# First stage of a fused decoder block: modulation columns loaded in blocks that pair shift and scale, tiles scaled and multiplied block by block

## What is computed

```python
c_act = jax.nn.silu(c)
mod = c_act @ w_mod[l] + b_mod[l]                 # 1024 -> 6 * 1024
sh1, sc1, g1, sh2, sc2, g2 = jnp.split(mod, 6, axis=-1)
h = _modulate(_rmsnorm(x, norm1_gain[l]), sh1, sc1)   # xhat * gain * (1 + sc1) + sh1
...
proj = h @ w_in                                   # 1024 -> 2372 columns
# index scores: idx_q @ idx_k, relu, weighted by idx_w, summed over 4 heads; top 256 keys of each query
# stick-breaking attention (8 heads), sparse attention (8 heads, the kept keys), output projection
x = x + g1 * mixer(h)
h = _modulate(_rmsnorm(x, norm2_gain[l]), sh2, sc2)
x = x + g2 * _swiglu(h, w_gate, w_up, w_down)
return _modulate(_rmsnorm(x, final_gain), sh_f, sc_f)
```

## Time and profile before

| | us |
|---|---|
| median of 3 runs | 1480.56 (1479.33 to 1481.61) |
| the profiled execution | 1475.04 |
| its span in the trace | 1473.3 |
| busy: PE, DVE, ACT, POOL | 1337.3, 1025.8, 680.1, 737.1 |
| mean granted TensorE clock | 0.964 of full |

### The profile page before, as it was taken

How to read it: one execution, slowest core, us unless ns; L and a number is a source line. 1 busy time by engine, 2 the same in 40 slices (tenths; PEclk the granted TensorE clock), 3 DMA queues, 4 the chain that set the end, 5 groups by cost and what they waited for, 6 DMA issues and landing times.

```text
span 1473.3 us, 18364 instructions
## 1 busy us (share of the span) xinstructions
PE 1337.3 (91%) x6085; PEld 1057.6 (72%) x6085; DVE 1025.8 (70%) x1478; ACT 680.1 (46%) x1132; POOL 737.1 (50%) x677
## 2 busy tenths in 40 slices
PE   1689999995999998895998899999999999999997
PEld 1556888784666666563886678888888888887885
DVE  4858579999677655543476997666666666477787
ACT  4435577744677655553213833332333334254332
POOL 1153355464456568875001245555555556487552
PEclk9798899996999999997899999999999999999999
DMA  8680134445444233220664245444444446889432
GB/s 335 191 225 18 58 129 135 136 157 151 113 115 115 57 110 85 72 60 22 256 210 134 76 141 184 150 149 152 152 156 161 156 150 219 321 297 322 166 114 115
DMA packets 124265, 223.33 MB, mean 152 GB/s; under 512 B 9322, under 2 KB 52436, under 8 KB 123924
## 3 DMA queue, kind: packets, MB, share of 16 engines
q1 hardware_dynamic: 124180, 222.27, 45.8%
HBM read 160.90 MB, written 57.93 MB: 149 GB/s over the span
## 4 chain that ended last, share of the span: by engine, by line
PE 41%; DVE 7%; issue 2%; DMA 1%; ACT 1%; POOL 0%; DVEq 0%; POOLq 0%; ACTq 0%
PE ps_out L2196 25%; PE ps_out L2222 12%; PE ps_out L1533 2%; PE ps_out L1549 1%; DVE mod_acc_final L1616 1%; DMA scr_mod_final<-mod_acc_final 1%; DVE y_full L1637 1%; DVE wgu_lo L2303 0%; ACT square_junk L2114 0%; DVE x L2458 0%; DVE y_gated L1649 0%; DVE down_part L2456 0%; DVE h_sum_t L2270 0%; DVE h_t_full L2270 0%; DVE x L2480 0%
## 5 line engine op out<-in xcount | busy, mean ns | idle before, releaser
L1893 POOL TENSOR_TENSOR wgu_lo<-wgu_raw,wgu_hi 128x512 fp32r<-128x512 f32 x66 | 97.2, 1481 | 127.7 <-ACT wgu_hi L1885 127.7
L2130 POOL TENSOR_TENSOR dn_lo<-dn_raw,dn_hi 128x512 fp32r<-128x512 f32 x77 | 126.3, 1658 | 67.7 <-ACT dn_hi L2036 67.7
L1885 ACT ACTIVATE wgu_hi<-wgu_sum 128x512 fp32r<-128x512 f32 x88 | 55.2, 632 | 199.0 <-DVE wgu_sum L2286 80.0
L2196 PE MATMUL ps_out<-h_b_t_hi,wgu_hi 128*128 128x512 f32 x352 | 137.9, 392 | 6.6 <-DVE h_b_t_lo L2274 2.7
L2196 PE MATMUL ps_out<-h_b_t_hi,wgu_lo 128*128 128x512 f32 x352 | 137.7, 391 | 0.0
L2196 PE MATMUL ps_out<-h_b_t_lo,wgu_hi 128*128 128x512 f32 x352 | 137.6, 391 | 0.0
L2036 ACT ACTIVATE dn_hi<-dn_raw 128x1024 fp32r<-128x1024 f32 x77 | 81.2, 1062 | 114.4 <-PE ps_out L2222 55.4
L413 POOL TENSOR_TENSOR win_lo<-win_raw,win_hi 128x256 fp32r<-128x256 f32 (+1 forms) x84 | 62.2, 771 | 136.5 <-ACT win_hi L404 136.5
L2222 PE MATMUL ps_out<-dn_hi 128*128 128x512 f32 x308 | 120.2, 390 | 0.0
L2222 PE MATMUL ps_out<-dn_hi,dn_lo 128*128 128x512 f32 x308 | 119.8, 389 | 0.0
L2222 PE MATMUL ps_out<-dn_lo,dn_hi 128*128 128x512 f32 x308 | 119.8, 389 | 0.0
(11 more groups left out here) (326 smaller groups left out, 3659.1 us busy)
## 6 DMA issues: line engine op xcount, KB each, us to landing
scr_act_sums<-act_sums SPq DMA_DIRECT2D x11, 1792.0 KB, 6.8
dn_raw<-scr_act_sums SPq DMA_DIRECT2D x77, 256.0 KB, 5.2
wgu_raw<-in_w_gate_dram SPq DMA_DIRECT2D x11, 1024.0 KB, 5.3
wgu_raw<-in_w_up_dram SPq DMA_DIRECT2D x11, 1024.0 KB, 5.3
wd_sums<-in_w_down_dram SPq DMA_DIRECT2D x11, 1024.0 KB, 5.0
scr_wd_sums<-wd_sums SPq DMA_DIRECT2D x11, 1024.0 KB, 4.1
dn_raw<-scr_wd_sums SPq DMA_DIRECT2D x44, 256.0 KB, 7.0
win_raw<-in_w_in_dram SPq DMA_DIRECT2D x20, 512.0 KB, 4.4
```

The lines of the kernel that those rows point to most:

```text
L1893: pool.tensor_tensor(sl[slot(m, x)][:], src, sh[slot(m, x)][:].bitcast(F32), ALU.subtract).then_inc(wlp, 1)
L2130: pool.tensor_tensor(bl[q % NSLOT][:, 1], braw[entry(q)][:, 1], bh[q % NSLOT][:, 1].bitcast(F32), ALU.subtract).then_inc(dlw, 1)
L2196: last = pe.matmul(bank(m, b), a[s][:, t], h[x][t // 2][:, t % 2], start=(fresh and t == 0 and a is sh and h is hh), stop=(t == 3 and a is ...
```

## The change

The blocks of `w_mod` are cut anew: block j now holds 256 columns of the shift and the same 256 features' scale, so that two feature groups can be scaled once one block is summed. A block arrives as two pieces of rows 0 to 5 of the eight slabs (`KV_` = 6) and two of rows 6 and 7, each with 256 columns. DVE's chain covers six slabs; PE takes the last two with eight more matmuls of one column against `csil` (`column_sums`). ACT makes the factors of each block from PSUM (`factors`, four operations of one column) instead of DVE. The `x` tiles 0 to 3 and the first two column tiles of `w_in` are loaded ahead of all blocks. The sixteen steps run in another order (`steps`), four of them ahead of blocks 2 and 3 on DVE, with three transpose buffers instead of four. The 16 steps of `mod_acc_early` leave the loop and stand behind it, with the other 16. Tile 2 of `w_in` is split into buffers of its own (`win2_hi`, `win2_lo`), its rounding on ACT is moved into the first stage, and its load and that of tile 3 stand ahead of `load_mod(0)`. Block buffer 0 now lies in `score`, so `load_mod(0)` waits for block 2.

```diff
-        for j in range(4):
+        def load_x(half):
+            for i in range(4 * half, 4 * half + 4):
+                sp.dma_start(xt[:, i, :], xb[i]).then_inc(x_loaded[i], 16)
+
+        def load_columns(j):
             if j >= 2:
-                for i in range(4 * j - 8, 4 * j - 4):
-                    sp.dma_start(xt[:, i, :], xb[i]).then_inc(x_loaded[i], 16)
                 sp.wait_ge(accd, j - 1)
-            sp.dma_start(wm[j % 2][:], w_mod[:, :, 512 * j:512 * j + 512]).then_inc(wm_loaded[j % 2], 16)
+                sp.wait_ge(modm, j - 1)
+            for t0, t1, done in ((0, KV_, wm_loaded), (KV_, KD, wp_loaded)):
+                for x in range(2):
+                    c = D * x + 256 * j
+                    sp.dma_start(wm[j % 2][:, t0:t1, 256 * x:256 * x + 256],
+                                 w_mod[:, t0:t1, c:c + 256]).then_inc(done[j % 2], 16)
+
+        load_x(0)
         then.first_loads(sp)
+        load_columns(0)
+        load_columns(1)
+        load_x(1)
+        load_columns(2)
+        load_columns(3)
...
+        then.first_highs(act)
+        factors(0)
+        modulate(0)
+        modulate(1)
+        square(4)
+        square(5)
+        factors(1)
+        modulate(2)
+        modulate(3)
+        square(6)
+        square(7)
         for i in range(4, NT):
             normalise(i)
-        then.first_highs(act)
-        for n in range(2 * KD):
+        factors(2)
+        for n in range(4, 12):
+            modulate(n)
+        factors(3)
+        then.third_high(act)
+        for n in range(12, 2 * KD):
             modulate(n)
...
+        column_sums(0)
+        for n in range(NTS):
+            transposes(n)
+        column_sums(1)
+        for n in range(2 * KD):
+            then.first_products(pe, n, *steps[n])
+            if n == 3:
+                column_sums(2)
+            if n + NTS < 2 * KD:
+                transposes(n + NTS)
+            if n == 5:
+                column_sums(3)
         pe.wait_ge(const_ready, 7)
-        for n in range(2 * KD):
-            if n + 4 < 2 * KD:
-                transposes(n + 4)
-            then.first_products(pe, n)
...
+        column_chain(0)
+        column_chain(1)
+        for n in range(4):
+            split(n)
+        column_chain(2)
+        column_chain(3)
+        for n in range(4, 2 * KD):
+            split(n)
         dve.wait_ge(const_ready, 7)
...
         def first_loads(sp):
-            sp.wait_ge(before.accd, 3)
             for n in range(2):
                 load_weights(sp, 0, n)
...
+            load_weights(sp, 0, 2)
+            load_weights(sp, 0, 3)
+            sp.wait_ge(before.accd, 3)
+            sp.wait_ge(before.modm, 3)
             load_mod(0)
             load_mod(1)
-            load_weights(sp, 0, 2)
-            load_weights(sp, 0, 3)
             for n in range(2, 7):
                 load_mod(n)
             stack_q(0)
...
             for n in range(3):
-                weights_high(act, 0, n + 2)
+                if n:
+                    weights_high(act, 0, n + 2)
                 evac(0, n, 0.125 if n < 2 else 1.0)
...
-            for m in range(2 * KD, 4 * NF):
+            for m in range(4 * NF):
                 modulation_step(dve, m)
```

More of the change, by code:

```diff
@@ L205, in normalise, with factors @@
             act.activation(xt[:, i, :], xt[:, i, :], ACT.Copy, scale=rstd[:, i:i + 1]).then_inc(xh, 1)
+        def factors(j):
+            act.wait_ge(modm, j + 1)
+            if j == 0:
+                act.wait_ge(abp, 1)
+            for t in range(2 * j, 2 * j + 2):
+                m = ps_m[:, 4 * j + t % 2:4 * j + t % 2 + 1]
+                act.activation(g.b1[:, t:t + 1], m, ACT.Identity, bias=g.cols[:, t:t + 1]).then_inc(ab, 1)
+                m = ps_m[:, 4 * j + 2 + t % 2:4 * j + 3 + t % 2]
+                act.activation(g.a1[:, t:t + 1], m, ACT.Identity, bias=ab1[:, t:t + 1],
+                               scale=g.cols[:, R_N1 + t:R_N1 + t + 1]).then_inc(ab, 1)
         def modulate(n):
-            t = n % KD
+            half, t = steps[n]
             act.wait_ge(tr, n + 1)
-            act.wait_ge(ab, 2)
+            act.wait_ge(ab, 4 * (t // 2 + 1))
             if n >= 2:
                 act.wait_ge(los, n - 1)
-            act.activation(hf[:, n % 2], ps_t[:, n % 4], ACT.Identity,
+            act.activation(hf[:, n % 2], ps_t[:, n % NTS], ACT.Identity,
                            bias=g.b1[:, t:t + 1], scale=g.a1[:, t:t + 1]).then_inc(hfs, 1)
@@ L235, in transposes, with column_sums @@
         def transposes(n):
-            half, t = n // KD, n % KD
+            half, t = steps[n]
             pe.wait_ge(xh, 4 * half + 4)
-            if n >= 4:
-                pe.wait_ge(hfs, n - 3)
+            if n >= NTS:
+                pe.wait_ge(hfs, n - NTS + 1)
             for i in range(4):
-                m = pe.transpose(ps_t[:, n % 4, P * i:P * i + P],
+                m = pe.transpose(ps_t[:, n % NTS, P * i:P * i + P],
                                  xt[:, 4 * half + i, P * t:P * t + P], g.ident[:])
             m.then_inc(tr, 1)
-        for n in range(4):
-            transposes(n)
-        for j in range(4):
-            pe.wait_ge(accd, j + 1)
-            for t in range(4):
-                m = pe.matmul(ps_m[:, 4 * j + t:4 * j + t + 1], acc[:, j, P * t:P * t + P],
-                              g.ones[:, 0:1], start=(j == 0 and t == 0), stop=True,
-                              skip_group_check=True)
-            m.then_inc(modm, 1)
+        def column_sums(j):
+            if j == 0:
+                pe.wait_ge(csil_ready, 1)
+            else:
+                pe.wait_ge(ab, 4 * j)
+            pe.wait_ge(wp_loaded[j % 2], 32 * (j // 2 + 1))
+            for t in range(KV_, KD):
+                for c in range(4):
+                    pe.matmul(ps_m[:, 4 * j + c:4 * j + c + 1], wm[j % 2][:, t, P * c:P * c + P], g.csil[:, t:t + 1],
+                              start=(j == 0 and t == KV_ and c == 0), stop=True, skip_group_check=True)
+            pe.wait_ge(accd, j + 1)
+            for c in range(4):
+                m = pe.matmul(ps_m[:, 4 * j + c:4 * j + c + 1], acc[:, j, P * c:P * c + P], g.ones[:, 0:1],
+                              start=False, stop=True, skip_group_check=True)
+            m.then_inc(modm, 1)
+        column_sums(0)
+        for n in range(NTS):
+            transposes(n)
+        column_sums(1)
[7 more added lines that the diff above has]
+                column_sums(3)
         pe.wait_ge(const_ready, 7)
-        for n in range(2 * KD):
-            if n + 4 < 2 * KD:
-                transposes(n + 4)
-            then.first_products(pe, n)
     def vector(dve):
@@ L401, in weights_high @@
             act.wait_ge(raw_loaded[n % 2], i * 8 + 16 * (n // 2 + 1))
+            if n == T_IKW:
+                act.activation(w2h[:, :, 0:w], raw[:, n % 2, :, 0:w], ACT.Copy).then_inc(whi, 1)
+                return
             if n >= 2:
@@ L409, in weights_low @@
             pool.wait_ge(whi, i + (n + 1))
-            if n >= 2:
+            if n >= 2 and n != T_IKW:
                 pool.wait_ge(proj, i + (n - 1))
+            high, low = (w2h, w2l) if n == T_IKW else (wh[:, n % 2], wl[:, n % 2])
             for t in range(0, KD, 2):
-                last = pool.tensor_tensor(wl[:, n % 2, t:t + 2, 0:w], raw[:, n % 2, t:t + 2, 0:w],
-                                          wh[:, n % 2, t:t + 2, 0:w].bitcast(F32), ALU.subtract)
+                last = pool.tensor_tensor(low[:, t:t + 2, 0:w], raw[:, n % 2, t:t + 2, 0:w],
+                                          high[:, t:t + 2, 0:w].bitcast(F32), ALU.subtract)
             last.then_inc(wlo, 1)
         def first_loads(sp):
-            sp.wait_ge(before.accd, 3)
             for n in range(2):
@@ L678, in project @@
                 s, m = n % 2, width(n)
-                tile_products(pe, ps_p[0:m, s], wh[:, s, :, 0:m], wl[:, s, :, 0:m], g.hTh, g.hTl).then_inc(proj, 1)
+                high, low = (w2h, w2l) if n == T_IKW else (wh[:, s], wl[:, s])
+                tile_products(pe, ps_p[0:m, s], high[:, :, 0:m], low[:, :, 0:m], g.hTh, g.hTl).then_inc(proj, 1)
             project(0, 2)
```

62 lines of the change are left out of this document (31 added, 31 removed).

## The result

The changed kernel is slower. Its median is 1490.3 us (1488.6 to 1492.9) beside 1480.3 (1479.3 to 1481.6) for the kernel before: a ratio of 1.0069, 95% interval 1.0051 to 1.0086. The profiled executions took 1488.6 and 1475.0, with spans of 1486.9 and 1473.3.

A forecast was written before the change was run, and what follows sets the result against it. DVE's key selection bounds the end, its start set by ACT's first relu (111.32). Tile 4 landing at 104.1 instead of being rounded at 93.06 adds 11.0 us: 1480.56 + 11.0 = 1491.6 us; range 1483.5 to 1498.0.

The forecast's parts named there:

- Packets of 1 KB: First-stage block transfers: 354 GB/s, between 289 and 398; last block's slabs 0 to 5 landed at 43.4 us.
- The third rival: First-stage blocks come at the rate of small packets, 289 GB/s: 5.0 us more, 1496.6 us; 15 in 100.
- The last chain ends at 47.8: DVE's last block sum ends at 47.8 us instead of 46.3; step 4 starts on PE at 48.9.
- The steps 0 to 3 fit on PE between 33 and 43: First stage on PE: the first four steps were taken to fit between 33 and 43 us.
- The cover that I had put at 3 us: Squares and normalising of tokens 512 and up end near 45 us, 3 us ahead of need.
- The other steps on PE: PE's steps 4 to 15 take 20.6 us, last `column_sums` 2.7, slow-clock start 1.2; PE ends at 73.4.
- The early sum: DVE's 32 steps begin at 71.3 us, behind the last split; piece 6 is issued at 92.2, 12.3 us later.
- Tile 4: Tile 4 of `w_in`, queued behind piece 6 on SP, lands at 104.1 us; the chain begins 11 us later.
- Tile 4 to relu: From ACT's rounding of tile 4 to its first relu: stays 18.3 us, putting the relu at 122.4.
- The first rival: PE still gates tile 4: relu up to 7.7 us earlier, 1472.9 us, faster; one in ten.
- the second (made up downstream): Rival: the delay is made up after the relu, in DVE's slack in the search: 1480.6 us, same; 5 in 100.
- frees nothing there: Taking early steps out of the split loop saves no time, since PE's pace of 1.83 us was the slower.

The follow-up runs named there:

- steps_in_loop: Changed kernel with 14 of the 16 moved early steps put back between the splits: 1480.5 us, ratio 1.0011 to the kernel before.
- transpose3_early: Changed kernel with PE's transposes for step 3 ahead of the products of step 0: 1491.9 us, ratio 1.0081 to the kernel before.
- first two attempts at a cure: tile4_first and both_cures, which issue loads of `w_in` tiles earlier on SP: 1493.0 and 1477.3 us.
- three later orders tried here: tile4_first, after_queue and kidx_first, the changed kernel with other orders on SP's queue: 1493.0, 1488.3 and 1492.2 us.
- tile4_first: Changed kernel with the load of tile 4 of `w_in` moved ahead of `load_mod(2)` on SP: 1493.0 us, ratio 1.0095 to the kernel before.
- kidx_first: Changed kernel with after_queue's order on SP, but tile 5 and `double_k` ahead of pieces 6 and 7: 1492.2 us, ratio 1.0089.
- both_cures: steps_in_loop with tile 4 ahead of `load_mod(4)` and tile 5 ahead of `load_mod(7)`, `stack_q(1)` and `double_k` on SP: 1477.3 us, ratio 0.9995.
- early_stack: steps_in_loop with SP reordered: tile 4 ahead of piece 4, `stack_q(0)` ahead of piece 6, tile 5 and `stack_q(1)` ahead of piece 7: 1473.9 us.
- after_queue: Changed kernel with only SP's order changed, `stack_q(0)` and tile 4 ahead of pieces 4 and on: 1488.3 us, ratio 1.0060.
- before_steps_out: Kernel before with one part of the change alone, all 32 early steps behind the last split: 1493.9 us, ratio 1.0114.
- before_tile5_first: Kernel before with the load of tile 5 of `w_in` ahead of `double_k()` on SP: 1474.9 us, ratio 0.9970.
- early_stack_t3: early_stack plus the edit of transpose3_early: 1470.9 us, ratio 0.9960 to the kernel before.

## Why the prediction was right, and where it was not

Forecast 1491.6, measured 1490.3, inside the range, and slower as said. By its steps:

- **Packets of 1 KB**: 354 GB/s taken, 347 to 350 read in the timeline's stretches of after (34 to 36 us: 349, share 1.11). The last block's rows were there by about 44, forecast 43.4: DVE waits for them in steps_in_loop and starts at 44.08, and starts without a wait at 43.88 in transpose3_early. The third rival (the rate of 512-byte packets) is out. So is, once more, the rule of the Trainium skill ("DMA: Bandwidth & Descriptors", Specifications) that 512 bytes reach the line rate: 289, 349 and 398 GB/s for 512 bytes, 1 KB and 2 KB are three different rates in these two kernels.
- **"The last chain ends at 47.8", "The steps 0 to 3 fit on PE between 33 and 43"**: this is the step that failed. The chain ended at 49.87 and step 4 started at 51.23 instead of 48.9. I had looked at block 3's landing and at PE's room, not at DVE's own queue: chain 2 stands behind split 3, and that waited for a scaling whose transposes stood on PE behind the half-rate products of step 0. Moving four instructions took 1.6 of these 2.1 us away; the other 0.5 is the block, which landed that much later than said. The cover that I had put at 3 us was gone as well: ACT normalised the last tile of `x` at 48.3, not near 45, and split 4 waited 0.15 us for ACT behind chain 3.
- **The other steps on PE**: 24.5 us from step 4 on (20.6 + 2.7 + 1.2), measured 24.9 (51.23 to 76.1).
- **The early sum**: from the last split to piece 6, 20.9 us forecast (71.3 to 92.2), 20.7 measured (73.90 to 94.6). This was the longest sum of the prediction and it is right to 0.2 us.
- **Tile 4**: 11.9 us from piece 6's issue to the rounding, measured 12.6.
- **Tile 4 to relu**: 18.3 against 18.1. **Relu to the end**: 1:1 (1362.0 us before, 1361.5 after).

In the traces the relu is 14.0 us late where I had 11.0: 2.3 for step 4 and 0.7 for tile 4, with the small misses of the other terms (+0.4, -0.2 and -0.2) cancelling. In the medians the difference is 10.0. So the nearness of 1491.6 to 1490.3 is in part luck: two errors of 3 and 4 us with opposite sign. The second is the spread between executions of one kernel (before: 1475.0 in the profiled one, 1479.3 to 1481.6 in the others). The traces show some of it where nothing is changed: from the start of the search to the end it is 1334.3 to 1342.3 us in the twelve kernels.

The first rival (PE still gates tile 4) is refuted by the releaser at 107.24; the second (made up downstream) by the equal distance from the search to the end. What no part of the prediction had is the second gate, `e_hi(0, 2)` behind the copies of `stack_q(0)`. It did not move the number, since both hang on piece 6 and tile 4 was the later one; it cost me the first two attempts at a cure. I had also written that taking the steps out of the loop "frees nothing there" and was right, but had not drawn the other half from the row of 56 to 76 us: the steps in the loop were what kept the transfers running there.

## What to carry to other kernels

A step that frees a buffer is worth more than its duration: before moving it off a busy engine, follow what is issued when it ends and what stands behind that issue on an in-order queue. Count the gates of the late instruction one by one, since opening one of two shows next to nothing (1.6 us of 14 here); and look at what the transfers do in the stretch that the step leaves, because if they stand idle there, the bytes have to go through later, and none of the three later orders tried here made up for that. Before calling an edit of a few microseconds a failure, see whether the clock of the profiled execution fell in a place where that of the other kernel did not.

## What the hardware showed that I had not expected

- PE's granted clock fell a second time, between 58 and 64 us, in some kernels (from 60 to 64 it reads 0.50 in tile4_first, 0.57 in kidx_first and both_cures, 0.62 in early_stack, 0.73 in after_queue, 0.81 in steps_in_loop) and not in others (1.00 in before, before_steps_out, before_tile5_first, after, transpose3_early and early_stack_t3), with PE busy in the trace all the time since 52 in every one where it fell. It costs up to some 4 us (tile 2 at 80.64 in tile4_first against 76.70 in after). What sets it off is not settled.
- PE ran at half its rate from 30 to 40 us of after, though the granted clock of that stretch reads 1.00: the 16 tiny matmuls of `column_sums` took 3.41 us at 30.46 and 1.84 at 44.77, and a product of 512 columns 0.63 at 36 and 0.39 at 42. Here the durations tell the rate and the column does not. In steps_in_loop the column does follow: it reads 0.55 from 34 to 36, where the products take 0.63 too.
- Copies within the on-chip memory fill the transfer engines out of proportion. In the kernel before, from 85 to 88 us, nearly all that travels is `stack_q`, in packets of 4 KB, at 199 GB/s with the engines at a share of 0.97 (the row below); loads in 2 KB packets ran at 398 with a share of 1.04. By these two a byte of a copy costs some 1.9 times as much as one of a load. The pieces of 1 MB, which took 5.4 us to land in after, took 9.3 in after_queue and 11.6 in kidx_first, where such copies and tiles of `w_in` are queued between them; how much of that is due to the copies is not shown.

```profile
DMA packets 175, 0.60 MB, mean 199 GB/s; under 512 B 29, under 2 KB 29, under 8 KB 175
```
